# Overflow tables in nine pieces over nine written-out blocks, one row spread moved behind the first gathers, 14 short products ahead of the recurrence's maps

## What is computed

```python
xn = rms_norm(h, norm_mix_g);  proj = xn @ w_in
o_att  = moba_attention(q, k, v, slopes)          # 8 heads x 64
o_rwkv = rwkv7_time_mix(proj[..., 1536:], ...)    # 8 heads x 64: state = state*w + sa*b + v*k, token by token
h = h + concat(o_att, o_rwkv) @ w_out
logits = rms_norm(h) @ w_router + b_router        # 32 experts
top_val, top_idx = top_k(logits, 4); gates = softmax(top_val)
for each expert e, each block of its tokens:
    gate = min(x @ w_gate[e] + b_gate[e], 7); up = clip(x @ w_up[e] + b_up[e], -7, 7)
    y = ((up + 1) * gate * sigmoid(1.702*gate)) @ w_down[e] + b_down[e]
h = h + sum of y * gate over a token's four experts
return rms_norm(h, norm_final_g)
```

## Time and profile before

| what | us |
|---|---|
| three runs, median | 1576.26 |
| three runs, lowest and highest | 1575.21, 1577.01 |
| the profiled execution | 1575.18 |
| its span, first to last instruction | 1573.5 |
| PE busy in it | 1519.9 (97%) |
| DVE busy | 1319.8 (84%) |
| ACT busy | 1085.5 (69%) |
| POOL busy | 607.2 (39%) |

### The profile page before, as it was taken

The page is one execution under the profiler, slowest core; times in us unless marked ns, Lnnn a source line. Parts: engine busy times, 40 slices in busy tenths (PEclk is TensorE's granted clock), DMA queues, the critical chain, the costliest instruction groups (busy, mean ns, idle before and its releaser), DMA issues.

```text
span 1573.5 us, 29685 instructions
## 1 busy us (share of the span) xinstructions
PE 1519.9 (97%) x10581; PEld 1250.5 (79%) x10581; DVE 1319.8 (84%) x1458; ACT 1085.5 (69%) x1316; POOL 607.2 (39%) x373
## 2 busy tenths in 40 slices
PE   7999987889999999999999999999999999999997
PEld 6877766776888788888888888888888888888884
DVE  4246456554699999999999999999999999999996
ACT  4245531103478888788888878888888888888874
POOL 7000312101031234345545655554355555444543
PEclk9999998998999999999999999999999999999999
DMA  7321110001699999999999999999999999999994
GB/s 239 98 68 41 40 41 4 4 4 67 232 369 375 388 393 375 396 367 398 390 378 388 394 392 394 393 383 374 385 391 392 392 390 385 381 377 393 393 391 146
DMA packets 81275, 464.35 MB, mean 295 GB/s; under 512 B 11642, under 2 KB 12854, under 8 KB 33072
## 3 DMA queue, kind: packets, MB, share of 16 engines
q1 hardware_dynamic: 71424, 438.68, 70.7%
q0 software_dynamic: 9104, 24.52, 6.8%
q10 hardware_dynamic: 672, 0.07, 0.0%
HBM read 449.16 MB, written 23.13 MB: 300 GB/s over the span
## 4 chain that ended last, share of the span: by engine, by line
PE 84%; DVE 10%; DMA 2%; issue 2%; ACT 1%; POOL 0%; POOLq 0%; SPq 0%; DVEq 0%; ACTq 0%
PE banks L381 69%; DVE expert_w_lo L321 5%; PE banks L1843 5%; PE banks L1936 1%; DMA expert_w_raw<-in_moe_w_gate_dram 1%; PE banks L2041 1%; PE banks L1920 1%; PE banks L2091 1%; DMA gate_bias_rows<-in_moe_b_gate_dram 1%; PE banks L2106 1%; DMA expert_w_raw<-in_moe_w_down_dram 1%; PE banks L2118 1%; PE banks L2503 0%; PE banks L2369 0%; PE banks L2109 0%
## 5 line engine op out<-in xcount | busy, mean ns | idle before, releaser
L321 DVE TENSOR_TENSOR expert_w_lo<-expert_w_raw,expert_w_hi 128x1024 fp32r<-128x1024 f32 x764 | 906.7, 1249 | 25.7 <-ACT expert_w_hi L316 25.4
L316 ACT ACTIVATE expert_w_hi<-expert_w_raw 128x1024 fp32r<-128x1024 f32 x764 | 749.2, 1056 | 27.6 <-DMA expert_w_raw<-in_moe_w_down_dram 21.9
L381 PE MATMUL banks<-expert_w_hi,x_block_T_hi 128*128 128x512 f32 x1008 | 395.8, 393 | 1.7 <-DVE expert_w_lo L321 1.5
L381 PE MATMUL banks<-expert_w_lo,x_block_T_hi 128*128 128x512 f32 x1008 | 392.6, 389 | 0.0
L381 PE MATMUL banks<-expert_w_hi,x_block_T_lo 128*128 128x512 f32 x1008 | 392.2, 389 | 0.0
L745 POOL COPY scatter_gates<-slot_gate 128x1 f32 x26 | 222.0, 8540 | 250.4 <-DMA y_sums<-y_block,scatter_rows 250.4
L381 PEld LDWEIGHTS banks<-expert_w_hi,x_block_T_hi 128*128 128x128 f32 x1008 | 189.3, 188 | 41.9 <-issue 1.9
L381 PEld LDWEIGHTS banks<-expert_w_lo,x_block_T_hi 128*128 128x128 f32 x1008 | 189.2, 188 | 39.9
L381 PEld LDWEIGHTS banks<-expert_w_hi,x_block_T_lo 128*128 128x128 f32 x1008 | 189.4, 188 | 38.0
L381 PE MATMUL banks<-expert_w_hi,h_block_T_hi 128*128 128x512 f32 x528 | 209.4, 397 | 2.0 <-DVE expert_w_lo L321 1.3
L381 PE MATMUL banks<-expert_w_lo,h_block_T_hi 128*128 128x512 f32 x528 | 205.9, 390 | 0.0
(11 more groups left out here) (399 smaller groups left out, 1949.8 us busy)
## 6 DMA issues: line engine op xcount, KB each, us to landing
expert_w_raw<-in_moe_w_up_dram SPq DMA_DIRECT2D x128, 1024.0 KB, 7.5
expert_w_raw<-in_moe_w_down_dram SPq DMA_DIRECT2D x128, 1024.0 KB, 9.6
expert_w_raw<-in_moe_w_gate_dram SPq DMA_DIRECT2D x126, 1024.0 KB, 9.8
w_raw<-in_w_in_dram SPq DMA_DIRECT2D x24, 512.0 KB, 3.8
residual<-in_x_dram SPq DMA_DIRECT2D x8, 512.0 KB, 4.9
w_raw<-in_w_out_dram SPq DMA_DIRECT2D x8, 512.0 KB, 3.3
staged_raw<-in_moe_w_gate_dram SPq DMA_DIRECT2D x2, 1024.0 KB, 6.1
y_sums<-residual SPq DMA_DIRECT2D x4, 512.0 KB, 7.4
```

The lines of the kernel that those rows point to most:

```text
L316: act.activation(self.hi[:, k % self.nhl, 0:width], self.raw[:, slot, 0:width], ACT.Copy)\
L321: dve.tensor_tensor(self.lo[:, k % self.nhl, 0:width], self.raw[:, (k - self.staged) % self.nraw, 0:width], self.hi[:, k % self.nhl, 0:wid ...
L381: last = pe.matmul(o, lhs, rhs, start=start and t == 0, stop=stop and t == 2, skip_group_check=preset)
```

## The change

Three things, all in the order of work; what is computed stays the same.

- `LOOP0` goes from 7 to 10: blocks 1 to 9 are written out, and the pieces of `over_part` are divided anew over them (counting of blocks; running sum and comparison; products with the one-hot; their sum; rounding; the row one-hot in two halves; the comparison of blocks; the reading of the sums). In the last of them the piece stands four low halves later. PE's slot sums move from block 6 to block 9 and wait for one `pairs_ok` more, since there are two halves.
- The broadcast of `spread_ready` moves from the recurrence to the place behind the gathers for blocks 1 and 0.
- `keep_warm`, new: PE multiplies `head_ones` (128 x 128) with 224 columns of `scan_mult` into columns 256 to 479 of PSUM bank 2, which nobody reads, 5, 5, 4 and 0 times at the start of `back_maps` of tiles 0 to 3.
- The orders of ACT and SP are unchanged.

```diff
--- before.py
+++ after.py
@@ -39,7 +39,8 @@
     NPAR = 17
     ROW0 = -1000.0
     PAIR_OF = (2, 3, 0, 1)
-    LOOP0 = 7
+    WARM, WARM_N = (5, 5, 4, 0), 224
+    LOOP0 = 10
 
     x_d = t_in["x"][0]
     w_in_v = t_in["w_in"][0].rearrange("(p k) n -> p k n", k=KT)
@@ -675,7 +676,6 @@
                 stage_r(n)
                 stage_bonus(n)
             ch.link(pool.memset(spread_ready[:, :], 0.0))
-            ch.link(pool.partition_broadcast(spread_ready[:, :], spread_ready[0:1, :], channels=P))
 
 
             for h in range(HP):
@@ -780,6 +780,7 @@
                 out=gate0[:, :], out_offset=None, in_=xn2_d,
                 in_offset=bass.IndirectOffsetOnAxis(ap=idx_x[:, 0:1].bitcast(U32), axis=0), element_offset=D,
                 bounds_check=last_x, oob_is_err=False).then_inc(S("gates0_in"), 16)
+            ch.link(pool.partition_broadcast(spread_ready[:, :], spread_ready[0:1, :], channels=P))
             pool.wait_ge(S("gates0_in"), 16)
             ch.link(pool.tensor_copy(slot_gate[:, 0:1], gate0[:, 0:1]))
 
@@ -1257,9 +1258,12 @@
                 lo(0, 8)
             hT_lo(dve, i - 1)
             lo(8, 14)
-            if isinstance(i, int):
+            if isinstance(i, int) and i < LOOP0 - 1:
                 over_part(i)
-            lo(14, 21)
+            lo(14, 18)
+            if isinstance(i, int) and i == LOOP0 - 1:
+                over_part(i)
+            lo(18, 21)
             up_part(dve, i, base_of(i) + 16)
             lo(21, 23)
             if final:
@@ -1758,28 +1762,31 @@
                         ins = dve.tensor_scalar(nbv[:, b, :], counts[:, :], float(P * b) if b else -1.0, None, ALU.is_gt)
                     ch.link(ins)
                     ch.link(dve.reduce_sum(nbl[:, :], nbv[:, :, :].rearrange("p b e -> p e b"), AXX))
+                elif i == 2:
                     ch.link(dve.tensor_tensor_scan(bend[:, :], onesf[:, :], nbl[:, :], 0.0, ALU.mult, ALU.add))
                     dve.tensor_copy(n_blk[:, 0:1], bend[:, NE - 1:NE])
                     dve.tensor_scalar(n_blk[:, 1:2], bend[:, NE - 1:NE], -4.0, None, ALU.add)
                     ch.link(dve.tensor_tensor(over[:, :], bend[:, :], iota32[:, :], ALU.subtract))
                     ch.link(dve.tensor_scalar(ecmp[:, :], over[0:NBT, :], iotaP[0:NBT, 1:2], None, ALU.is_le))
                     ch.link(dve.tensor_tensor(over[:, :], over[:, :], nbl[:, :], ALU.subtract))
-                elif i == 2:
+                elif i == 3:
                     ch.link(dve.tensor_tensor(dovr[:, :, :], OH[:, :, :, :].rearrange("p t k e -> p (t k) e"),
                                               bc(over[:, :], [P, NP, NE], 1), ALU.mult))
+                elif i == 4:
                     ch.link(dve.reduce_sum(dover[:, :], dovr[:, :, :], AXX))
-                elif i == 3:
+                    ch.link(dve.tensor_scalar(dfull[:, :], dest[:, :], 1.0 / P, (-ROW0 - (P - 1) / 2) / P, ALU.mult, ALU.add))
+                elif i == 5:
                     MAGIC = 1.5 * 2.0 ** 23
-                    ch.link(dve.tensor_scalar(dfull[:, :], dest[:, :], 1.0 / P, (-ROW0 - (P - 1) / 2) / P, ALU.mult, ALU.add))
                     for shift in (MAGIC, -MAGIC):
                         ch.link(dve.tensor_scalar(dfull[:, :], dfull[:, :], shift, None, ALU.add))
                     ch.link(dve.scalar_tensor_tensor(destr[:, :], dfull[:, :], -float(P), dest[:, :], ALU.mult, ALU.add))
                     ch.link(dve.scalar_tensor_tensor(dmore[:, :], dfull[:, :], 1.0, dover[:, :], ALU.min, ALU.mult))
                     ch.link(dve.tensor_tensor(destb[:, :], dmore[:, :], dfull[:, :], ALU.add))
-                elif i == 4:
-                    dve.tensor_tensor(ohR[:, :, :], bc(destr[:, :], [P, NP, P], 2), bc(iotaR[:, :], [P, NP, P], 1),
+                elif i in (6, 7):
+                    ms = slice((i - 6) * (NP // 2), (i - 5) * (NP // 2))
+                    dve.tensor_tensor(ohR[:, ms, :], bc(destr[:, ms], [P, NP // 2, P], 2), bc(iotaR[:, :], [P, NP // 2, P], 1),
                                       ALU.is_equal).then_inc(S("pairs_ok"), 1)
-                elif i == 5:
+                elif i == 8:
                     ch.link(dve.tensor_tensor(dcmp[:, :, :], bc(destb[:, :], [P, NP, NOV], 2),
                                               bc(iotaB[:, 1:1 + NOV], [P, NP, NOV], 1), ALU.is_equal))
                     dve.tensor_scalar(rhso[:, 0], dcmp[:, :, :], iotaP[:, 2:3], None, ALU.mult)
@@ -2119,9 +2126,14 @@
                                          AZ[n % 2][half(c), k, :, :].rearrange("p u d -> p (u d)"), start=True, stop=True)
                 last.then_inc(S("uz_ps"), 1)
 
+            def keep_warm(count):
+                for k in range(count):
+                    pe.matmul(bank[IV[0]][:, 256:256 + WARM_N], head_ones[:, :], SCM[:, 0:WARM_N], start=True, stop=True)
+
             def back_maps(n):
                 b = n % 2
                 nxt = min(n + 2, TT)
+                keep_warm(WARM[n])
                 pe.wait_ge(S("uz_rows"), n + 1)
                 pe.wait_ge(S("uz_rows_b"), n + 1)
                 pe.wait_ge(S("RB_ok"), n + 1)
@@ -2456,7 +2468,7 @@
                     chunk(base + (8 + c), UP0 + 8 + c, pair[1], xbh, xbl, c)
                     if c == 3 and isinstance(i, int) and i == LOOP0 - 1:
                         pe.wait_ge(S("hT_ok"), i)
-                        pe.wait_ge(S("pairs_ok"), TT + 2)
+                        pe.wait_ge(S("pairs_ok"), TT + 3)
                         flip(bank[6][0:1, 0:NBT], bef[:, :], NBT)
                         slot_sums(rhso, NOV)
                 if not (isinstance(i, int) and i == 1):
```

## The result

| | us, median (lowest to highest, runs) | profiled execution | its span |
|---|---|---|---|
| before | 1576.45 (1573.73 to 1580.77, 19) | 1575.18 | 1573.5 |
| with the change | 1580.55 (1576.85 to 1586.33, 19) | 1580.21 | 1578.5 |

The ratio is 1.0025, 95% interval 1.0016 to 1.0033: **slower by 4 us**, where 1575.5 was forecast and the range ended at 1580.0. The two profiled executions differ by 5.0. Mean granted clock of both: 0.988.

A forecast was written before the change was run, and what follows sets the result against it. PE was taken to set the pace of the expert blocks, DVE 3% behind. On the profiled 1575.18 us, +5.6 - 1.5 - 4.9 = -0.8 gave 1574.4, plus 1.1 for the median 1575.5; range 1572.3 to 1580.0 us.

The forecast's parts named there:

- Products +5.6: Recurrence: the 14 products ahead of the maps lie uncovered on the chain, 0.40 us each, +5.6 us.
- One fall saved, -1.5: Recurrence joints: the products avoid one of two clock falls, each costing 1.5 us, so -1.5 us.
- rival 2: Recurrence: clock falls move elsewhere, so products +5.6, nothing saved, blocks -4.9: +0.7 us, 1577.0; chance 0.22.
- Row spread: cost nothing: POOL behind the gathers: the moved load delays the next gather about 1 us, with over 15 to spare; cost nothing.
- its gain of 0.91: Block 3: the load's 6.14 us gone, ACT no longer waits at the bias row and DVE gains 0.91 us.
- rival 5: Row spread: load moves its wait to the second gather or is needed again at first bias row; about 1577.4; chance 0.03.
- Blocks -4.9: Expert blocks 1 to 6: of 5.9 us of stalls, DVE's later pieces and the reload return 4.9 us.
- The slot wait's 1.2: Block 6: of 1.3 us lost behind the wait for PE's slot sums, moving them to block 9 returns 1.2.
- The 3.7 of blocks 1 to 5: Expert blocks 1 to 5: of 4.6 us lost, DVE's earlier finish returns 3.7 us.
- rival 1: Blocks 2 and 3: weights, not DVE, are late; blocks give 2.0, no fall saved: +3.6 us, 1579.9; chance 0.18.
- the recorded signs of being wrong: Products under 0.35 us each or hidden, over two falls fewer in 240 to 350, or 3 us stalls in blocks 2 to 5.
- Written-out blocks nothing: Expert blocks: three more written-out blocks cost nothing by themselves, at most a few tenths for longer code.

The follow-up runs named there:

- e1: The kernel before with the 14 short products ahead of the maps alone; 1582.72 us, ratio 1.0041 to the kernel before.
- g3: The changed kernel with PE's code for overflow blocks (and its branch) left out; 1582.38 us, ratio 1.0027 to the kernel before.
- g4: The changed kernel with twice the products (10, 10 and 8) and PE's code for overflow blocks left out; 1586.46 us, ratio 1.0057 to the kernel before.
- e2: The changed kernel without the 14 products, row spread and pieces kept; 1579.37 us, ratio 1.0027 to the kernel before.
- e3: The kernel before with the row spread moved behind the gathers alone; 1575.44 us, ratio 0.9994 to the kernel before.
- g1: The kernel before with PE's code for overflow blocks (and its branch) left out; 1577.22 us, ratio 1.0007 to the kernel before.
- g2: The changed kernel without the 14 products and without PE's code for overflow blocks; 1574.36 us, ratio 0.9985 to the kernel before.
- h2: The kernel before with the nine pieces and LOOP0 = 10 only, PE's code for overflow blocks left out; 1575.36 us, ratio 0.9991 to the kernel before.
- h3: The kernel before with LOOP0 = 10 and the old pieces, PE's code for overflow blocks left out; 1576.25 us, ratio 0.9994 to the kernel before.
- i1: The changed kernel without the 14 products, a repeat of e2; 1577.46 us, one run.
- e4: The kernel before with the 14 products put behind the maps; 1576.33 us, ratio 1.0000 to the kernel before.
- h4: The changed kernel with its 14 products behind the maps, nothing left out; 1573.27 us, ratio 0.9982 to the kernel before.
- i2: The changed kernel with 3, 2 and 2 products behind the maps; 1580.91 us, ratio 1.0028 to the kernel before.
- h1: The kernel before with 32 one-column products behind the maps of each of tiles 0 to 2; 1613.13 us, ratio 1.0222 to the kernel before.

## Why the prediction was wrong

The median came 5.0 above the forecast. Two terms of its sum were wrong by their mechanism: the clock (1.5 forecast as saved, on balance nothing) and the blocks (2.6 short). A cost of some 1.2 was missing, and the products were 0.3 cheaper. 1.5 + 2.6 + 1.2 - 0.3 is the 5.0.

By its own steps:

- **Products +5.6: right as PE time, 5.3** (0.378 each, not 0.40), on the chain, uncovered. Right too that DVE's work moves with them.
- **One fall saved, -1.5: the first step that failed.** Two things were wrong in it. First, the products keep nothing up. They stand ahead of the maps, while the idle time is behind them, as the text itself said; with products in front 1, 2, 3 and 4 falls (after, e1, g3, g4) began between `back_UZ` of tile 0 and the group norm, without them 2, 2, 0, 0, 2, 0, 1 and 3 (before, e2, e3, g1, g2, h2, h3, i1). That is what rival 2 said, and the Trainium skill's free-running monitor ("TensorE: Matmul & The Clock Gate", Part 1), by which the term was 0: the traces agree, since the same 14 products ahead were followed by falls at the third joint alone (after), at the first two (e1) or at all three (g3). Work in the idle time itself is another matter: with products behind the maps no fall began there in three of three profiles (e4, h4, i2), where the recorded reading had that no place is made safe for good. Three are few, though: three of the eight without products had none either. Second, a fall that goes is not worth its whole price, since at the full clock PE runs into gaps named issue, which end with its instruction packets (above). For that stretch, of each profile, with the time at the low clock and the sum of PE's issue gaps over 0.25 us:

| kernel | stretch | low clock | issue |
|---|---|---|---|
| before | 101.9 | 9.1 | 3.0 |
| e2 | 101.5 | 9.1 | 2.2 |
| i1 | 102.9 | 12.4 | 2.7 |
| g2 | 102.5 | 9.0 | 3.5 |
| e3 | 99.1 | 0 | 4.3 |
| h2 | 99.4 | 0 | 3.6 |
| g1 | 102.9 | 0 | 6.7 |
| h3 | 105.1 | 5.7 | 7.5 |
| e4, products behind | 101.3 | 0 | 5.9 |
| h4, products behind | 103.7 | 2.5 | 7.6 |
| i2, half behind | 102.8 | 0 | 7.8 |
| after, products ahead | 107.4 | 3.4 | 5.6 |
| e1, products ahead | 107.4 | 6.8 | 4.0 |
| g3, products ahead | 109.4 | 10.2 | 4.5 |

  95.5 us, plus the issue gaps in full, plus 0.35 of the time at the low clock, plus 5.3 where products stand ahead, gives every row within 0.7 (a fit of mine; g2 and i2 were not in it and come out within 0.5). It is not for g4, which it misses by 0.8, or for h1, whose products did not fit the idle time. By it the kernel after saved 2.0 on the clock against before and gave 2.6 back in issue gaps. The eight profiles with no product anywhere average 101.9, the three with 14 ahead 108.1: **+6.2**, as e1's median has it.
- **A further 1 us that no step had.** PE's code became longer by the products' own instructions, which shifts where the instruction packets fall, and an issue gap appeared in tile 3's last group, a joint without a product in it. In the chain after:

```profile
358.72 0.70 PE banks L2167 x48
359.42 0.76 issue
360.18 0.46 PE banks L2167 x16
```

  In the kernel before the same 64 products take 0.93 without one. From `back_UZ` of tile 3 to the group norm it is 12.6 us in all eight profiles without products and 13.6 to 14.4 in all eight with any, ahead or behind.
- **Row spread: cost nothing, right; its gain of 0.91 never came** (e3: median -0.8, blocks no shorter). In the kernel after, DVE's 0.91 became a wait of 0.93 for ACT in block 1, and in e3 ACT waited for the second bias row, which is near what rival 5 had as "needed again at the first bias row".
- **Blocks -4.9, measured -2.3: the second step that failed.** The slot wait's 1.2 is right: 36.65 us from swish 6 to 7 before, now 34.46 there and 35.51 from 9 to 10, so -1.1. The 3.7 of blocks 1 to 5 measured 1.2. The prediction put all 4.6 that these blocks lose down to DVE's own work, as PE's stalls name DVE's low halves; but DVE itself stood there, 2.8 us in block 2 behind ACT and the weights, in the kernel before. This is the mechanism of rival 1: the weights of block 2 are as late as before, and the time that DVE has over ahead of them is waited away. From the swish of block 1 to that of block 3 it stood the same 3.7 us (on average over the profiles 3.4 without the pieces, 4.3 with them). From the swish of block 1 to that of block 6 there are still 3.35 us lost against the pace; stalls of 3 us and more left there were among the recorded signs of being wrong.
- **Written-out blocks nothing: right for the blocks** (h3), but they move the branch behind the loop in the code, and without the products it then costs 6.6 (e2, i1).

Rival 1's sum was +5.6 and -2.0, 1579.9; the median is 0.65 above it. The doubt that was noted there (it decides once the blocks give under 2.4) was the right one to weigh more. Against the kernel before, -2.4 (g2) and +6.5 (e1) are +4.1, and +4.1 was measured by medians, 3.9 by the ratio, so the parts add up; g3, after without the branch, is level with it by the ratio (1.0027 and 1.0025), so the branch costs the changed kernel nothing that could be told.

## What to carry to other kernels

Work that is to keep PE's clock up must stand in the idle time itself, behind what starts the wait, and be no longer than it: the same 14 products cost 6.5 us ahead of the maps and nothing behind them. Even there they bought nothing, so show first that the clock is what binds: look for issue gaps in a stretch where the clock stays up. Where one engine's late blocks have two causes, freeing one engine gives only what the other leaves (a gain of 3.7 by DVE's budget was 1.2 beside late weights), and after any change of code length read the jumps behind a loop before the medians of its parts are added.

## What the runs showed of the hardware

- **A forward jump on PE behind a hardware loop took 0.36 or 4.7 to 5.2 us**, with a stretch at the low clock behind it, 6.1 to 7.2 us in all. All four slow branches are in profiles whose last instruction packet for PE ahead of the branch came within 5 us of the swish of the loop's first block; in all six quick ones (before, after, e1, e4, h1, h4) a later one came, 15 to 155 us behind that swish. The slow branches end 1.5 us behind the end of the packet that comes during them. In h1 PE stopped a few instructions behind a quick branch, for 4.4 us, and that stop too ends 1.6 us behind a packet's end. By this timing PE waits there for its instructions; why the later packet comes in some executions of the same PE program (before) and not in others (e3) is open.
- **In the recurrence PE runs near the pace at which its instructions come**: 27 packets of 16 KB in 120 us, and gaps of 0.3 to 1.6 us whose place moves with the length of the code. All 112 of them in sixteen profiles end 1.2 to 1.7 us behind the end of a packet, which waits for other engines do not. h1, which should have shown it by its time, did not.
- A float32 product of one column with a 128 x 128 weight took 105 ns a record at full clock, against 189 for 224 columns.
- The first use of POOL's broadcast stood 10.3 us behind the gathers (9.9 to 11.4 in the nine profiles with it there), against 6.14 at the first bias row and 5.6 to 6.1 in the recurrence (seven profiles).
